# Routing weights by a one-hot product, and expert rows added into the stream by the fetches, in a two-layer kernel on one core

## The chip, the cores and the metric

The kernel runs on one core of one Trainium2 chip. The metric is the device time of one execution in microseconds. A core has TensorE (PE in the profile), VectorE (DVE), ScalarE (ACT), GpSimd (POOL) and SyncE (SP); SP, ACT and POOL issue DMAs, which all run on the core's 16 DMA engines.

## The reference, cut to what matters

Two different layers run one after the other over 1024 tokens of width 1024, in float32. The first ends in a mixture of experts with 16 experts in 4 groups; each token takes one group and two experts of it. The second begins with an RMS norm and the product with `w_in_2`.

```python
e_val = e_val / jnp.sum(e_val, -1, keepdims=True)
combine = one_hot(g_idx[:, 0], 4)[:, :, None] * g_val[:, :, None] * w_group[:, None, :]
hid = jax.nn.silu(gate) * up * combine[..., None]
moe = jnp.einsum('tef,efd->td', hid, w_down)
x = layer_norm(alpha * x + g_f * moe, ln2_g, ln2_b)       # end of the first layer
u = rmsnorm(x, norm_mix_2) @ w_in_2                       # start of the second
```

`g_f` is a row of 1024 gates that all tokens share; `alpha` is 2 to the power 1/4.

## The kernel before

The stream `x1` (tile arena_b) holds 8 tiles of 128 tokens by 1024. Each engine runs its own program, written out by hand in functions named after the engine, and the order on an engine is the order of the calls; between engines there are semaphores.

**The expert stage.** The router gives every token two places, one for each of its experts, in a list of 24 blocks ("slots") of 128 rows; a block belongs to one expert, or its two halves to two. `dve_router` works out the weights `w1` and `w2` (per token) and the places `posi`; `dve_inverse` and `pe_inverse` turn the places around by a product of two one-hot tables: `inv` names the token of each slot row. `pool_rows` fetches the rows of a block by an indirect DMA from a copy of the stream in DRAM, three blocks ahead (L1883). For each block TensorE turns the rows (L1954), multiplies by gate and up (L1966), turns the hidden tile (L1975) and multiplies by down (L1987). VectorE multiplies the result in PSUM by the gate row `rowg` (L2063), and ScalarE's queue stores it to `yslots` in DRAM (L2007). SP loads the experts' weights in three rotating buffers; the third gate and up buffer lies in arena_d, where the one-hot tables lie before, so SP waits for the tables' last use ahead of its third load (`if j == 2`).

**Adding the experts' rows.** When all blocks are stored, `pool_gather` fetches for each of the 8 token tiles the two rows of each token, 512 KB a fetch, into four buffers `g12` (L1896). ScalarE multiplies the second row by `w2` (L2104), VectorE adds the first times `w1` (L2159), then alpha times the stream (L2161). After that VectorE takes mean and variance (L1502 to L1505) and, one tile later, norms (L1510 to L1515), ScalarE sums squares (L2136), takes roots, and writes the normed tile `xr` (L2142), TensorE turns it (L1555), ScalarE copies it out (L2148). Meanwhile SP loads `w_in_2`, as soon as both rows of tile 1 are in (L2206), in two halves of 2 MB, and ScalarE multiplies each of their 16 pieces by `norm_mix_2` (L2117), two pieces a tile from the third turn of its loop on. In the second layer's first product (L2223) TensorE begins after the fifth turned tile and after the first eight pieces, one group of products a tile.

**GpSimd after that** builds tables for the second layer (`pool_tables`, L2604 to L2616), from the end of the last L2161 on.

## Time and profile before

| | us |
|---|---|
| median of 3 runs | 3191.38 (3189.43 to 3196.72) |
| the profiled execution, its own time | 3191.05 |
| its span in the profile | 3189.3 |
| PE busy | 2965.5 (93%) |
| DVE busy | 1505.0 (47%) |
| POOL busy | 1060.3 (33%) |
| ACT busy | 743.4 (23%) |
| mean granted TensorE clock | 0.961 |

The profile is of one execution. Its times count from the start of the span; 1.75 us of the execution lie outside it. Busy shares are means over stages with different limits: TensorE is full nearly everywhere, but two of its forty slices are low: the 21st (6 tenths), which holds the entry of the expert stage, and the 25th (2 tenths), which holds the addition of the experts' rows. A line such as "L2159 DVE" names the line of the kernel before. An indirect DMA of GpSimd shows as busy while its descriptors are written, not while data move.

### The profile page before, as it was taken

What the parts mean: (1) busy time and instruction counts of PE and PEld (TensorE: products, weight loads), DVE (VectorE), ACT (ScalarE), POOL (GpSimd) and SP (SyncE); (2) the same over time, 40 slices, a digit from 0 to 9 for tenths busy, and PEclk for the clock granted to TensorE, in tenths of its full rate; (3) what the DMA queues carried; (4) which work ended last, traced back from release to release, by engine and by line L of the source; (5) the groups of instructions that cost most, each with busy time, mean ns of one, the idle gap of its engine ahead of it and who ended that gap; (6) DMA issues with size and microseconds to landing.
All of it is one profiled execution on the core that took longest, in us unless ns stands there. A gap on an engine that the chain in (4) does not pass through costs nothing. (4 is left out here: it accounts for less than half of the span.)

```text
span 3189.3 us, 28756 instructions
## 1 busy us (share of the span) xinstructions
PE 2965.5 (93%) x10235; PEld 1480.4 (46%) x10235; DVE 1505.0 (47%) x2430; ACT 743.4 (23%) x1535; POOL 1060.3 (33%) x979
## 2 busy tenths in 40 slices
PE   7998999999899999999869992978999999999997
PEld 4554554444455555344534441565444444444443
DVE  2434882345666666322345327265132444444446
ACT  2213855411233333200111115222110000000002
POOL 0002870000376767500010003181022555555445
PEclk9998999999899999999979995998999999999998
DMA  7001322000100000111168964001020111211101
GB/s 268 20 0 52 88 79 96 27 27 19 34 1 1 1 1 1 54 33 37 49 252 339 391 269 165 4 14 53 0 79 27 40 40 40 73 46 40 40 14 60
DMA packets 128383, 229.14 MB, mean 72 GB/s; under 512 B 25288, under 2 KB 81264, under 8 KB 118384
## 3 DMA queue, kind: packets, MB, share of 16 engines
q1 hardware_dynamic: 117712, 197.72, 17.5%
q0 software_dynamic: 5760, 16.78, 1.4%
q10 hardware_dynamic: 4768, 12.79, 1.1%
q8 instruction: 82, 1.34, 0.2%
q14 instruction: 61, 0.50, 0.0%
HBM read 231.45 MB, written 22.03 MB: 79 GB/s over the span
## 5 line engine op out<-in xcount | busy, mean ns | idle before, releaser
L1366 DVE TENSOR_REDUCE arena_b<-ps 128x1 f32<-128x512 f32 (+1 forms) x384 | 217.6, 600 | 148.5 <-PE ps L1254 148.1
L3173 POOL TENSOR_TENSOR arena_b<-arena_b,arena_d 128x512 f32<-128x512 f32 x132 | 165.6, 1271 | 363.2 <-DVE arena_d L3353 362.2
L3325 DVE TENSOR_TENSOR arena_d<-arena_d,ps 128x512 f32<-128x512 f32 x154 | 101.8, 684 | 388.4 <-PE ps L3216 388.4
L1348 POOL TENSOR_TENSOR arena_b<-arena_b 128x512 f32<-128x512 f32 x182 | 224.5, 1268 | 96.6 <-ACT arena_b L1330 96.6
L1254 PE MATMUL ps<-arena_d,arena_a 64*128 64x512 f32 (+1 forms) x768 | 239.1, 548 | 3.7 <-DVE arena_b L1357 2.9
L1273 PE MATMUL ps<-arena_a,arena_d 64*128 64x512 f32 x640 | 220.0, 607 | 2.4 <-ACT arena_b L1330 1.8
L3350 DVE TENSOR_TENSOR arena_b<-arena_b,ps 128x512 f32<-128x512 f32 x264 | 174.3, 685 | 42.8 <-POOL arena_b L3173 27.4
L1077 PE MATMUL ps<-ring,arena_b 128*128 128x512 f32 x384 | 167.4, 592 | 0.0
L564 PE MATMUL ps<-arena_b,ring 128*128 128x512 f32 x384 | 167.1, 593 | 0.0
L1330 ACT ACTIVATE arena_b<-ps 128x512 f32<-128x512 f32 x214 | 116.2, 595 | 212.8 <-PE ps L1279 212.8
L3216 PE MATMUL ps<-arena_a,ring 128*128 128x512 f32 x352 | 155.1, 599 | 3.1 <-DMA ring<-in_w_up 3.1
L1254 PEld LDWEIGHTS ps<-arena_d,arena_a 64*128 64x128 f32 x768 | 115.2, 192 | 73.7 <-issue 42.5
L1966 PE MATMUL ps<-ring,arena_a 128*128 128x512 f32 (+1 forms) x352 | 144.2, 603 | 3.4 <-ACT arena_a L2014 3.4
L782 POOL TENSOR_TENSOR ring<-m_le,arena_t 128x512 f32<-128x512 f32 x32 | 40.7, 1271 | 285.8 <-ACT arena_d L654 282.1
L1348 POOL TENSOR_TENSOR arena_b<-arena_b,arena_t 128x512 f32<-128x512 f32 x96 | 118.8, 1269 | 46.1 <-ACT arena_t L1330 46.1
L1273 PEld LDWEIGHTS ps<-arena_a,arena_d 64*128 64x128 f32 x640 | 88.8, 185 | 79.4 <-issue 33.2
L3257 ACT ACTIVATE arena_d<-arena_d 128x512 f32<-128x512 f32 x44 | 27.8, 631 | 394.8 <-DVE arena_d L3325 394.8
L3237 PE MATMUL ps<-arena_c,arena_t 128*128 128x512 f32 x240 | 116.0, 592 | 0.0
L1484 PE MATMUL ps<-ring,arena_c 128*128 128x512 f32 x256 | 113.2, 595 | 0.0
L988 PE MATMUL ps<-ring,arena_b 128*128 128x512 f32 x256 | 112.3, 593 | 0.8 <-DVE arena_a L729 0.8
L564 PEld LDWEIGHTS ps<-arena_b,ring 128*128 128x128 f32 x384 | 72.0, 190 | 86.0 <-issue 86.0
L1077 PEld LDWEIGHTS ps<-ring,arena_b 128*128 128x128 f32 x384 | 71.7, 190 | 84.2 <-issue 84.2
(571 smaller groups left out, 5325.8 us busy)
## 6 DMA issues: line engine op xcount, KB each, us to landing
ring<-in_w_gate SPq DMA_DIRECT2D x33, 1024.0 KB
ring<-in_w_up SPq DMA_DIRECT2D x33, 1024.0 KB
ring<-in_w_down SPq DMA_DIRECT2D x33, 1024.0 KB
ring<-in_w_in SPq DMA_DIRECT2D x10, 2048.0 KB, 15.6
ring<-in_w_mod SPq DMA_DIRECT2D x32, 512.0 KB, 3.9
yslots<-arena_a ACTq DMA_DIRECT2D x24, 512.0 KB
arena_d<-in_w_gate SPq DMA_DIRECT2D x10, 1024.0 KB
arena_d<-in_w_up SPq DMA_DIRECT2D x10, 1024.0 KB
```

The costliest lines, as they stand in the source:

```text
L564: mm = eng.matmul(ps[:, b, 0:n], w[:, k, (m % 4) * P:(m % 4 + 1) * P], src[:, k, :], start=(k == 0), stop=(k == KT - 1))
L1077: mm = eng.matmul(ps[:, 2 * (j % 2) + n, :], h_tile(k, t), w[:, k, :], start=(k == 0), stop=(k == KT - 1))
L1254: eng.matmul(ps[:, shared("s", u), 0:k1 - k0], qT[rows, pr, q0:q0 + P], kT[rows, pr // 2, k0:k1], start=True, stop=True).then_inc(s_S, 1)
L1273: eng.matmul(ps[:, 3 + (n + e) % 3, :], kT[rows, pr // 2, kt * P:(kt + 1) * P], qT[rows, pr, qs], start=True, stop=False)
L1330: eng.activation(prT[n % NPR], ps[:, 3 + n % 3, :], ACT.Exp).then_inc(s_ex, 1)
L1348: eng.tensor_tensor(acc, first, prT[n % NPR], ALU.add).then_inc(s_pa, 1)
L1366: eng.tensor_reduce(mx3[j % 2][:, t, e, piece:piece + 1], ps[:, shared("s", u), 0:k1 - k0], AX.X, ALU.max).then_inc(s_mx, 1)
L1966: mm = eng.matmul(ps[c0:c1, s % 2, :], xsT[s % 2][:, k, c0:c1], sguw[j % 3][:, :, k, :], start=(k == 0), stop=(k == KT - 1))
L3173: eng.tensor_tensor(o, o, dsum[0 if a == "a12" else 1], ALU.add).then_inc(s_comb, 1)
L3216: mm = eng.matmul(bank_of("gu", b, w, p), lhs, rhs, start=(k == 0), stop=(k == HK - 1))
L3237: eng.matmul(bank_of("dn", b, i, p), lhs[p], rhs[p], start=True, stop=True).then_inc(dn_done, 1)
L3350: ins = eng.tensor_tensor(o, o, src, ALU.add)
```

## The change

The weights now enter at the experts' side. `dve_slot_weights` splits each token weight into three bfloat16 pieces and writes, for each piece, the one-hot table of blocks times the weight; `pe_slot_weights` multiplies by the one-hot table of rows (16 products that add up in one PSUM bank), and `dve_slot_weights_copy` adds the three pieces to `w_slot`, one weight for each slot row. The copy of a block's output (L2115 of after) multiplies by it and by the gate row in one instruction. SP's third load waits for the new product and not for `inv`.

The fetches write no buffers any more: each is an indirect DMA with an add, from `yslots` straight into the stream tile. GpSimd scales the eight stream tiles by alpha, one ahead of each of the row fetches 3 to 10. First rows of a tile are fetched three tiles ahead of second rows, since the two additions to one tile may not overlap. L2104, L2159 and L2161 are gone. SP's load of `w_in_2` still waits for both rows of tile 1, and GpSimd's tables now wait for the end of the expert products and the parameters alone.

```diff
+        def dve_slot_weights(eng):
+            place = Chain(eng, s_place, N_INV)
+            many = lambda v: v.rearrange("p j t n -> p (j t) n")
+            place(eng.tensor_copy(w_piece[0], w12))
+            place(eng.tensor_tensor(w_rest[0], w12, w_piece[0], ALU.subtract))
+            place(eng.tensor_copy(w_piece[1], w_rest[0]))
+            place(eng.tensor_tensor(w_rest[1], w_rest[0], w_piece[1], ALU.subtract))
+            place(eng.tensor_copy(w_piece[2], w_rest[1]))
+            for a in range(3):
+                place(eng.tensor_tensor(weight_of[:, :, a, :], many(slot_of), bc(w_piece[a], 2, NSLOT), ALU.mult))
+
+        def pe_slot_weights(eng):
+            eng.wait_ge(s_place, N_WT)
+            for j in range(2):
+                for t in range(LT):
+                    mm = eng.matmul(ps[:, 7, 0:3 * NSLOT], row_of[:, j, t, :],
+                                    weight_of[:, j * LT + t, :, :].rearrange("p a n -> p (a n)"),
+                                    start=(j + t == 0), stop=(j == 1 and t == LT - 1))
+            mm.then_inc(s_packT, 1)
+
+        def dve_slot_weights_copy(eng):
+            eng.wait_ge(s_packT, STRIP_SUM + NSTRIP + 4)
+            place(eng.tensor_copy(w_slot, ps[:, 7, 0:NSLOT]))
+            for a in (1, 2):
+                place(eng.tensor_tensor(w_slot, w_slot, ps[:, 7, a * NSLOT:(a + 1) * NSLOT], ALU.add))
...
         def pool_rows(eng):
+                if 3 <= n < 3 + LT:
+                    t = n - 3
+                    eng.tensor_scalar(x1[:, t, :], x1[:, t, :], ALPHA, None, ALU.mult).then_inc(s_gx, 1)
...
         def pool_gather(eng):
+            def rows_of(t, j):
+                return eng.indirect_dma_start(
+                    out=x1[:, t, :], out_offset=None, in_=yslots,
+                    in_offset=bass.IndirectOffsetOnAxis(ap=posi[:, j, t:t + 1], axis=0), compute_op=ALU.add)
+
+            eng.wait_ge(s_gx, LT)
             for i in range(2):
                 eng.wait_ge(ys_out[i], 16 * ((NSLOT + 1 - i) // 2))
-            for t in range(LT):
-                if t >= 4:
-                    eng.wait_ge(s_gx, t - 3)
-                for j in range(2):
-                    eng.indirect_dma_start(
-                        out=g12[t % 4][:, j, :], out_offset=None, in_=yslots,
-                        in_offset=bass.IndirectOffsetOnAxis(ap=posi[:, j, t:t + 1], axis=0)
-                    ).then_inc(g_in[t % 4], 16)
+            for u in range(LT + YLAG):
+                if u < LT:
+                    rows_of(u, 0).then_inc(g_in[u % 4], 16)
+                if u >= YLAG:
+                    t = u - YLAG
+                    eng.wait_ge(g_in[t % 4], 16 * (t // 4 + 1))
+                    if t >= 3:
+                        eng.wait_ge(*second_rows(t - 3))
+                    rows_of(t, 1).then_inc(y_in[t % 3], 16)
...
                 if j == 2:
-                    eng.wait_ge(s_place, N_INV)
+                    eng.wait_ge(s_packT, STRIP_SUM + NSTRIP + 4)
...
-                eng.tensor_tensor(ysl[s % 2], ps[:, 5:7, :].rearrange("p a n -> p (a n)"), rowg, ALU.mult
-                                  ).then_inc(s_ye, 1)
+                eng.scalar_tensor_tensor(out=ysl[s % 2], in0=ps[:, 5:7, :].rearrange("p a n -> p (a n)"),
+                                         scalar=w_slot[:, ORDER[s]:ORDER[s] + 1], in1=rowg, op0=ALU.mult,
+                                         op1=ALU.mult).then_inc(s_ye, 1)
...
-        def act_second_row(eng, t):
-            eng.wait_ge(g_in[t % 4], 32 * (t // 4 + 1))
-            eng.activation(g12[t % 4][:, 1, :], g12[t % 4][:, 1, :], ACT.Identity, scale=w2[:, t:t + 1]
-                           ).then_inc(s_re, 1)
...
         def dve_x2(eng):
-                    g = g12[t % 4]
-                    eng.wait_ge(s_re, row_scaled(t))
-                    ch = Chain(eng, s_place, N_INV + t)
-                    ch(eng.scalar_tensor_tensor(out=g[:, 0, :], in0=g[:, 0, :], scalar=w1[:, t:t + 1], in1=g[:, 1, :],
-                                                op0=ALU.mult, op1=ALU.add))
-                    step(eng, eng.scalar_tensor_tensor(out=x1[:, t, :], in0=x1[:, t, :], scalar=ALPHA, in1=g[:, 0, :],
-                                                       op0=ALU.mult, op1=ALU.add), s_gx, t + 1)
+                    eng.wait_ge(*second_rows(t))
...
         def sp_second(eng):
-            eng.wait_ge(g_in[1], 32)
+            eng.wait_ge(*second_rows(1))
...
         def pool_tables(eng):
-            eng.wait_ge(s_gx, LT)
+            after(eng, "moe")
```

GpSimd's program where the experts' rows are fetched, before. "slot_rows_stored" is the landing of the blocks in DRAM, "experts_added" the end of an L2161.

```order
L1896 DMA arena_d<-yslots,arena_t 128x1024 [waits slot_rows_stored1,slot_rows_stored0]
L1896 DMA arena_d<-yslots,arena_t 128x1024 x3
L1896 DMA ring<-yslots,arena_t 128x1024 x4
L1896 DMA arena_d<-yslots,arena_t 128x1024 [waits experts_added]
L1896 DMA arena_d<-yslots,arena_t 128x1024
L1896 DMA arena_d<-yslots,arena_t 128x1024 [waits experts_added]
```

And in the changed kernel. "first_rows_added" is the landing of a first row, "slot_and_second_rows_loaded" that of a second.

```order
L1936 DMA arena_b<-yslots,arena_t 128x1024 [waits slot_rows_stored1,slot_rows_stored0,stream_tiles_scaled]
L1936 DMA arena_b<-yslots,arena_t 128x1024 x3
L1936 DMA arena_b<-yslots,arena_t 128x1024 [waits first_rows_added0]
L1936 DMA arena_b<-yslots,arena_t 128x1024
L1936 DMA arena_b<-yslots,arena_t 128x1024 [waits first_rows_added1]
L1936 DMA arena_b<-yslots,arena_t 128x1024
L1936 DMA arena_b<-yslots,arena_t 128x1024 [waits first_rows_added2]
```

The first four fetches are first rows of tiles 0 to 3; the second row of tile 1 was the fourth fetch and is the seventh, and fetches wait for fetches, not for VectorE.

VectorE's program in the same stage, tiles 1 and 2 (with the norm of tile 0), before:

```order
L2159 SCALAR_TENSOR_TENSOR arena_d<-arena_d,arena_t 128x1024 [waits router_act_steps,norm_steps]
L2161 SCALAR_TENSOR_TENSOR arena_b<-arena_b,arena_d 128x1024 [waits place_steps]
L1502 BN_STATS arena_d<-arena_b 128x6 [waits experts_added]
L1502 BN_STATS arena_d<-arena_b 128x6
L1504 BN_AGGR arena_d<-arena_d 128x2 [waits norm_steps]
L1505 TENSOR_SCALAR arena_d<-arena_d 128x1 [waits norm_steps]
L1510 RECIPROCAL arena_d<-arena_d 128x1 [waits conditions_and_roots,norm_steps]
L1513 SCALAR_TENSOR_TENSOR arena_b<-arena_b,arena_d 128x1024 [waits norm_rows_loaded,normed]
L1515 SCALAR_TENSOR_TENSOR arena_b<-arena_b,arena_d 128x1024 [waits normed]
L2159 SCALAR_TENSOR_TENSOR ring<-ring,arena_t 128x1024 [waits router_act_steps,normed]
```

And in the changed kernel:

```order
L1502 BN_STATS arena_d<-arena_b 128x6 [waits slot_and_second_rows_loaded1,norm_steps]
L1502 BN_STATS arena_d<-arena_b 128x6
L1504 BN_AGGR arena_d<-arena_d 128x2 [waits norm_steps]
L1505 TENSOR_SCALAR arena_d<-arena_d 128x1 [waits norm_steps]
L1510 RECIPROCAL arena_d<-arena_d 128x1 [waits conditions_and_roots,norm_steps]
L1513 SCALAR_TENSOR_TENSOR arena_b<-arena_b,arena_d 128x1024 [waits norm_rows_loaded,normed]
L1515 SCALAR_TENSOR_TENSOR arena_b<-arena_b,arena_d 128x1024 [waits normed]
L1502 BN_STATS arena_d<-arena_b 128x6 [waits slot_and_second_rows_loaded2,normed]
```

Two of the big instructions of a tile are gone, and the statistics wait for the DMA itself.

VectorE's program between its parameter steps and the first expert block, before:

```order
L2445 TENSOR_SCALAR arena_c<-arena_c 128x32 [waits s5_param_steps]
L2043 TENSOR_SCALAR arena_a<-ps,csil 128x128 [waits slot_rows_turned,rope_loaded,s5_param_steps]
L2043 TENSOR_SCALAR arena_a<-ps,csil 128x128 x3
L2051 TENSOR_TENSOR arena_a<-arena_a,ps 128x256 [waits silu_ready]
```

And in the changed kernel:

```order
L1728 CAST arena_d<-arena_t 128x16 [waits s5_param_steps]
L1729 TENSOR_TENSOR arena_d<-arena_t,arena_d 128x16 [waits place_steps]
L1730 CAST arena_d<-arena_d 128x16 [waits place_steps]
L1731 TENSOR_TENSOR arena_d<-arena_d 128x16 [waits place_steps]
L1732 CAST arena_d<-arena_d 128x16 [waits place_steps]
L1734 TENSOR_TENSOR arena_d<-arena_d 128x16x24 [waits place_steps] x3
L2095 TENSOR_SCALAR arena_a<-ps,csil 128x128 [waits slot_rows_turned,rope_loaded,place_steps]
L2095 TENSOR_SCALAR arena_a<-ps,csil 128x128 x3
L1749 COPY arena_t<-ps 128x24 [waits small_products]
L1751 TENSOR_TENSOR arena_t<-arena_t,ps 128x24 [waits place_steps] x2
L2103 TENSOR_TENSOR arena_a<-arena_a,ps 128x256 [waits silu_ready,place_steps]
```

Eight steps stand ahead of the first block's modulation and three behind it.

## Rows read from the trace of the kernel before

**Rows 1.** Stretches: start:end, length, busy (x) of PE, PEld, DVE, ACT, POOL; PEclk, DMA share, GB/s.
```profile
1915.00:1947.50 32.50, 0.00 (x0) 0.00 (x0) 20.54 (x29) 9.66 (x14) 13.15 (x14) 0.54 0.86 324
1947.50:1980.00 32.50, 9.84 (x40) 7.84 (x40) 31.02 (x48) 23.75 (x39) 2.95 (x8) 0.50 0.21 80
1980.00:2012.00 32.00, 31.67 (x88) 15.05 (x88) 6.74 (x14) 15.41 (x25) 21.94 (x38) 0.96 0.04 9
2012.00:2107.00 95.00, 94.32 (x248) 59.63 (x248) 25.94 (x28) 17.90 (x30) 30.07 (x68) 1.00 0.00 1
```

**Rows 2.** Waits of PE from 1622 to 2107: us in total, times, longest us.
```profile
PE ps L1555 <- ACT arena_t L2142: 55.8, 5, 33.5
```

**Rows 3.** Timeline of DVE, one tile: start us, us, line, operation [idle before].
```profile
1960.77 1.28 DVE L2159 SCALAR_TENSOR_TENSOR arena_d<-arena_d,arena_t 128x1024 f32<-128x1024 f32 x1
1962.08 1.23 DVE L2161 SCALAR_TENSOR_TENSOR arena_b<-arena_b,arena_d 128x1024 f32<-128x1024 f32 x1
1963.34 1.28 DVE L1502 BATCH_NORM_STATS2 arena_d<-arena_b 128x6 f32<-128x512 f32 x2
...
1968.32 1.28 DVE L2159 SCALAR_TENSOR_TENSOR ring<-ring,arena_t 128x1024 f32<-128x1024 f32 x1
```

**Rows 4.** Timeline of ACT and PE up to the second layer's first product.
```profile
1947.54 1.32 ACT L2117 ACTIVATE ring<-ring,cols 128x512 f32<-128x512 f32 x2
...
1964.78 1.15 ACT L2104 ACTIVATE ring<-ring,arena_t 128x1024 f32<-128x1024 f32 x1
...
1968.12 1.06 ACT L2136 ACTIVATE arena_t<-arena_b 128x1024 f32<-128x1024 f32 x1 [2.01 <-DVE arena_b L1515]
...
1980.04 8.44 PE L2223 MATMUL ps<-arena_a,ring 128*128 128x512 f32 x16 [0.15 <-ACT arena_a L2148]
```

**Rows 5.** Timeline of POOL and SP at the fetches, and landing of L1896.
```profile
1918.86 0.95 POOL L1896 DMA_INDIRECT arena_d<-yslots,arena_t  x1 [58.13 <-DMA yslots<-arena_a]
1920.12 0.95 POOL L1896 DMA_INDIRECT arena_d<-yslots,arena_t  x1 [0.30 <-issue]
...
1928.87 1.07 SPq L2208 DMA_DIRECT2D ring<-in_w_in  x2
...
DMA to landing us min/median/max: 4.2/6.3/8.3
```

**Rows 6.** DMA from 1930 to 1933, then 1933 to 1942; queues: packets, MB, share.
```profile
DMA packets 348, 1.20 MB, mean 399 GB/s; under 512 B 36, under 2 KB 36, under 8 KB 348
q1 hardware_dynamic: 39, 0.08, 6.8%
...
DMA packets 1317, 3.65 MB, mean 405 GB/s; under 512 B 64, under 2 KB 64, under 8 KB 1316
q0 software_dynamic: 588, 2.15, 60.1%
q1 hardware_dynamic: 728, 1.49, 43.2%
```

**Rows 7.** Timeline at the entry of the expert stage: DVE, PE and SP.
```profile
1607.19 1.15 DVE L1706 TENSOR_TENSOR arena_d<-arena_d 128x384 bf16<-128x384 f32 x2
1610.92 0.50 PE L1722 MATMUL ps<-arena_d 128*128 128x48 bf16 x8 [0.76 <-DVE arena_d L1708]
1613.08 0.34 SPq L1925 DMA_DIRECT2D arena_d<-in_w_gate  x1
1617.17 0.18 DVE L2445 TENSOR_SCALAR arena_c<-arena_c 128x32 f32<-128x32 f32 x1
1622.17 1.95 PE L1954 MATMUL ps<-ident,arena_a 128*128 128x128 f32 x8 [8.63 <-DMA arena_a<-x_dram,arena_t]
1638.17 0.62 PE L1966 MATMUL ps<-ring,arena_a 128*64 128x512 f32 x1 [1.69 <-ACT arena_a L2014]
```

**Rows 8.** Timeline of DVE beside POOL, and POOL's waits from 1625 to 1915.
```profile
1984.89 1.36 DVE L1513 SCALAR_TENSOR_TENSOR arena_b<-arena_b,arena_d 128x1024 f32<-128x1024 f32 x1
1997.75 1.04 POOL L2611 TENSOR_TENSOR ring<-ring,arena_c 128x512 f32<-128x512 f32 x1
...
POOL arena_a L1883 <- PE ps L1954: 223.3, 21, 13.2
```

More of the change, by code:

```diff
@@ L1667, in build @@
         inv = view(arena_t, 3440, NSLOT).bitcast(U32)
+        w12 = view(arena_t, 3864, 2 * LT)
+        w_piece = [view(arena_d, 3600 + 8 * i, 8).bitcast(BF16) for i in range(3)]
+        w_rest = [view(arena_d, 3632 + 16 * i, 2 * LT) for i in range(2)]
+        weight_of = view(arena_d, LT * P, 3 * LT * NSLOT).bitcast(BF16).rearrange("p (m a n) -> p m a n", a=3, n=NSLOT)
+        w_slot = view(arena_t, 3520, NSLOT)
+        N_WT = N_INV + 8
+        N_WS = N_WT + 3
         def pool_places(eng):
@@ L1716, in dve_inverse_copy @@
             place(eng.tensor_copy(posi, posf))
+        def dve_slot_weights(eng):
[8 more added lines that the diff above has]
+                place(eng.tensor_tensor(weight_of[:, :, a, :], many(slot_of), bc(w_piece[a], 2, NSLOT), ALU.mult))
+            assert place.n == N_WT
+        def pe_slot_weights(eng):
[7 more added lines that the diff above has]
+        def dve_slot_weights_copy(eng):
+            place = Chain(eng, s_place, N_WT)
+            eng.wait_ge(s_packT, STRIP_SUM + NSTRIP + 4)
+            place(eng.tensor_copy(w_slot, ps[:, 7, 0:NSLOT]))
+            for a in (1, 2):
+                place(eng.tensor_tensor(w_slot, w_slot, ps[:, 7, a * NSLOT:(a + 1) * NSLOT], ALU.add))
+            assert place.n == N_WS
         def pe_inverse(eng):
@@ L1863, in parts @@
                 [(LOADS.index((n, 0)), 0, P)]
-        g12 = [view(a, at, 2, D) for a, at in ((arena_d, 0), (arena_d, 2 * D), (ring, 2 * PAN), (ring, 2 * PAN + 2 * D))]
-        xs_in = [sem(f"slot_rows_loaded{i}") for i in range(3)]
+        xs_in = [sem(f"slot_and_second_rows_loaded{i}") for i in range(3)]
+        y_in = xs_in
         ys_out = [sem(f"slot_rows_stored{i}") for i in range(2)]
-        g_in = [sem(f"token_rows_gathered{i}") for i in range(4)]
+        g_in = [sem(f"first_rows_added{i}") for i in range(4)]
         s_xT, s_xe = sem("slot_rows_turned"), sem("slot_rows_modulated")
         s_hT, s_hTc = sem("slot_hidden_turned"), sem("slot_hidden_copied")
-        s_ye, s_gx = sem("slot_output_copied"), sem("experts_added")
+        s_ye, s_gx = sem("slot_output_copied"), sem("stream_tiles_scaled")
         ends["moe"] = [(dn_done, NSLOT)]
@@ L1887, in pool_rows, with second_rows @@
                 ).then_inc(xs_in[n % 3], 16)
+        YLAG = 3
+        def second_rows(t):
+            return y_in[t % 3], 16 * (NSLOT // 3) + 16 * (t // 3 + 1)
         def pool_gather(eng):
+            def rows_of(t, j):
[3 more added lines that the diff above has]
+            eng.wait_ge(s_gx, LT)
             for i in range(2):
                 eng.wait_ge(ys_out[i], 16 * ((NSLOT + 1 - i) // 2))
-            for t in range(LT):
-                if t >= 4:
-                    eng.wait_ge(s_gx, t - 3)
-                for j in range(2):
-                    eng.indirect_dma_start(
-                        out=g12[t % 4][:, j, :], out_offset=None, in_=yslots,
-                        in_offset=bass.IndirectOffsetOnAxis(ap=posi[:, j, t:t + 1], axis=0)
-                    ).then_inc(g_in[t % 4], 16)
+            for u in range(LT + YLAG):
[7 more added lines that the diff above has]
+                    rows_of(t, 1).then_inc(y_in[t % 3], 16)
         def sp_ln2(eng):
@@ L2062, in store @@
                     eng.wait_ge(ys_out[s % 2], 16 * (s // 2))
-                eng.tensor_tensor(ysl[s % 2], ps[:, 5:7, :].rearrange("p a n -> p (a n)"), rowg, ALU.mult
-                                  ).then_inc(s_ye, 1)
+                eng.scalar_tensor_tensor(out=ysl[s % 2], in0=ps[:, 5:7, :].rearrange("p a n -> p (a n)"),
+                                         scalar=w_slot[:, ORDER[s]:ORDER[s] + 1], in1=rowg, op0=ALU.mult,
+                                         op1=ALU.mult).then_inc(s_ye, 1)
+            dve_slot_weights(eng)
             eng.wait_ge(s_rope, 32 + 32)
             modulate(0)
+            dve_slot_weights_copy(eng)
             hidden(0)
@@ L2100, in build @@
         s_xr = sem("stream_normed")
-        def act_second_row(eng, t):
-            eng.wait_ge(g_in[t % 4], 32 * (t // 4 + 1))
-            eng.activation(g12[t % 4][:, 1, :], g12[t % 4][:, 1, :], ACT.Identity, scale=w2[:, t:t + 1]
-                           ).then_inc(s_re, 1)
-        def row_scaled(t):
-            return 2 + t + 1 + 2 * max(0, t - 3)
-        IN2_GAINED = (2 + LT - 1 + KT, 2 + LT + 2 * KT)
+        IN2_GAINED = (2 + KT, 2 + 2 * KT)
         def act_gains(eng, n, k):
@@ L2119, in act_x2 @@
         def act_x2(eng):
-            eng.wait_ge(s_place, N_PLACE)
-            act_second_row(eng, 0)
             for t in range(LT + 3):
-                if t + 1 < LT:
-                    act_second_row(eng, t + 1)
                 if t < LT:
@@ L3509, in _ @@
             pe_s5_params(eng)
+            pe_slot_weights(eng)
             pe_slots(eng)
```

## The prediction

> **What bounds the kernel now.** I read the stage table first, then the waits of TensorE, then the timeline of the one stretch that they point to. In the stage table [rows 1] TensorE does nothing from 1915.0 to 1947.5, works 9.84 of the next 32.5 us, and from 1980.0 on is full again (31.67 of 32.0, then 94.32 of 95.0). The waits say the same: 55.8 us in five pieces, 33.5 us the longest, all for ScalarE's L2142, which writes the normed stream [rows 2]. So between the last expert block and the first product of the second layer (L2223, 1980.04) time is set by something else, and whatever moves that product moves everything behind it, since TensorE hardly waits for 127 us after.
>
> Inside the gap two things matter. VectorE turns one tile every 7.55 us (L2159 at 1960.77 and again at 1968.32 [rows 3]), with no idle time between. And the DMA engines are full: at 405 GB/s from 1933 to 1942 [rows 6]. They carry 16 fetches of 512 KB (8.39 MB) and then w_in_2, twice 2.10 MB, which ScalarE must multiply by the norm gains (L2117) before TensorE may use it. L2117 first runs at 1947.54, without idle time ahead of it [rows 4]: before, those weights are in time.
>
> **What the change takes away.** On VectorE L2159 and L2161 go: start to start 1.31 and 1.26 us [rows 3], so a tile takes 7.55 - 2.57 = 4.98 us. On ScalarE L2104 (1.15 us a tile [rows 4]) goes. ScalarE's tile was its 7.55 less 2.0 of idle [rows 4], and is now some 4.5 us, still under VectorE. Were nothing else to change, four tile turns lie between the first gain and the first product (32.5 us = 4 x 7.55 + 2.3), so 10 us would go there, and some more ahead of it.
>
> **What the fetches now cost.** The two rows of a token are no longer copied into a buffer but added into the stream by the DMA. The trace has no adding DMA; its price is bounded by the plain fetch. 0.524 MB at the 399 GB/s of 1930 to 1933 [rows 6] is 1.31 us of all DMA engines. A plain fetch reads a row and writes a row. An added one reads two rows (the expert's and the stream's own) and writes one. If the second read is free it stays 1.31 us; if reading is the full side, it is 2.62; if the three passes follow each other, 3.93. I take 2.62: the plain fetch already keeps the engines full with one read, so the second needs the same time again. Both ends stay in the range. It can't be under 1.31, as no byte is saved.
>
> The Trainium skill bears on this (Collectives: The Full Stack, "The bandwidth ceiling: the fold count and why AG ≠ RS ≠ AR"): an add in the DMA reads two sources through the same read ring, and the measured collective with adds ran at about half the rate of the copying one. No row of this trace shows it. By that rule a fetch is 2.62 us and the time 3197, by the plain row 1.31 us and 3180 (both worked out below).
>
> **When w_in_2 arrives.** It is issued when both rows of tile 1 are in. Before, that was 1928.87, and its first bytes moved about 3.6 us later (39 packets by 1933 [rows 6]). Now tile 1's second row is the seventh fetch in GpSimd's new order (four first rows, then second and first rows in turn). The first fetch is issued at 1918.86 and a plain one lands after 4.2 at best [rows 5]; with 1.31 more it lands at 1924.4. Six more at 2.62 give 1940.1. First bytes: 1943.7. GpSimd's own issuing is no limit: 1.25 us a fetch [rows 5].
>
> Then w_in_2 shares the engines with the fetches that are left. In 1933 to 1942 it had 43.2% and the fetches 60.1% [rows 6], normed 42 to 58, with 728 packets of 2 KB against 588, most of 4 KB. So engines take packets from both queues nearly in turn, and a packet that costs double takes double: 42 to 116, or 27% for the weights. The Trainium skill (DMA: Bandwidth & Descriptors, "Queues, rings and completion order") says the same, that an engine goes round the queues packet by packet; the packet counts agree. The first half of w_in_2 needs 2.10 MB at 405 GB/s, 5.2 us, alone, so 19.3 us, and about 1 to land: **1964.0**. By then five more fetches have passed, tile 4's second row among them; the last row lands near 1972, and VectorE and ScalarE need it later than that.
>
> **From there to the product.** ScalarE is in order, so it stands at L2117 until 1964.0, and VectorE with it, one tile on, at the root that ScalarE would take next. From the first gain to the product: 4 x 4.98 + 2.3 = 22.2, less 1.2 since VectorE stands ahead: 21.0. First product: 1985.0, against 1980.04. **+5.0 us.**
>
> **Smaller terms.** GpSimd's tables (from L2604) waited for the last L2161 and now start once the last fetch is issued, beside VectorE's norms. Where they meet, L1513 takes 1.36 us and not 1.28, and large table steps take 1.04 [rows 8]. Eight to ten such meetings: +0.8. The store of an expert block takes a scalar more; only the last is on the path, +0.05. GpSimd scales eight stream tiles between row fetches, 1 to 2.5 us each by its 1.04 for half a tile [rows 8]. It waited 223.3 us in 21 pieces there [rows 8], 10.6 each, and rows are fetched three blocks ahead: nothing.
>
> At the entry VectorE has five small steps (0.2 each) and three products of 384 elements (0.57, as L1706) after its last parameter step at 1617.35: done at 1620.1. Then 16 small products on TensorE, 0.50 for eight narrower ones [rows 7], so 1.3: 1621.5. The first turn waits for its rows until 1622.17 [rows 7]. The row fetch covers it with 0.7 us to spare; with no cover at all it would cost the whole 4.2. SP is moved more: the third weight buffer, and down weights queued behind it, wait for those products, 1621.6 and not 1613.08. Its 2.10 MB at three quarters of the engines are in at 1631; TensorE takes them at 1638.17 [rows 7]. Nothing, with 7 us to spare.
>
> **Sum.** 3191.05 (the profiled execution, 0.33 under the median of the runs) + 5.0 + 0.8 + 0.1 = **3197**.
>
> **Rivals.**
> *An added fetch costs what a plain one does.* The first lands at 1923.1, the seventh at 1931, first bytes of w_in_2 at 1934.5, 5.2 / 0.42 = 12.4 and 1 more: 1947.9, product at 1968.9: 11 us less, **3180**. For it: writes are not more than before, and the full engines may be full on the writing side. Against it: two reads.
> *In between*, two reads partly beside each other, 1.97 a fetch: first in at 1923.7, seventh 1935.5, bytes 1939.1, share 42 to 87 or 33%, weights at 1955.9, product at 1977: **3189**, and 3183 to 3194 on either side.
> *Half rate, but the queues share time, not packets:* weights at 1957; now the rows are late, 4.5 us a fetch, tile 6 complete near 1974, product near 1983: **3194**. Against it the packet counts.
> *Slower for certain: an added fetch costs more than two reads.* At 3.93: first in at 1925.7, seventh 1949.3, bytes 1952.9, share 42 to 174 or 19%, weights in 27 + 1 us later at 1980.7, product 2001.7: **3213**. From about 2.7 us a fetch on, the loss passes 0.2%. A variant is that the issue itself grows past 2.6 us on GpSimd.
> *The change doesn't do what it says:* the weighting isn't hidden at the entry, TensorE's small products or the third weights come late and hold the first two blocks. That adds 1 to 7 to the sum: 3198 to 3204.
>
> **How the numbers follow.** Half rate in either sharing 0.42 (3194 to 3200, 3197 likeliest), copy rate 0.24 (3180), between 0.14, above half 0.16 (3201 to 3225), the entry 0.04. A measurement of this kernel can tell about 0.2%, 6.4 us. Faster than that: the copy rate and half of the between, 0.31. Slower: all above half, 0.35 of the half-rate case and the entry, 0.34. Within: 0.35. The range reaches from the copy rate, 3179, to three passes, 3213.
>
> **What the profile after would show.** VectorE's tile turns at 4.98 us once nothing waits. The queue of GpSimd: about 200 GB/s alone, 400 if the first rival holds. The landing of an added fetch: 5.5 us for the first. w_in_2 issued near 1940. ScalarE idle ahead of its first gain, ended by a DMA, until about 1964. First product of the second layer at 1985, and the stretch behind it as long as before. If ScalarE isn't idle ahead of the gain, the DMA term is wrong and the time is near 3180; if VectorE waits for rows on every tile, it is above 3200.

## The result and the profile after

| | before | after |
|---|---|---|
| median of 5 runs, us | 3194.38 (3189.43 to 3197.63) | 3207.61 (3205.43 to 3210.08) |
| the profiled execution, us | 3191.05 | 3205.43 |
| mean granted TensorE clock | 0.961 | 0.959 |

The changed kernel takes 1.0044 times as long (95% interval 1.0032 to 1.0055): slower by some 13 to 14 us, where the prediction had 6 (3197 against 3191.05).

The waits of TensorE from 1700 to 2000 (us in total, times, longest) and the stretches of the core, with the columns of [rows 1]:

```profile
PE ps L1555 <- ACT arena_t L2184: 69.3, 5, 39.8
```

```profile
1915.00:1970.40 55.40, 1.97 (x8) 1.57 (x8) 16.19 (x29) 5.44 (x11) 30.58 (x41) 0.53 0.95 212
1970.40:1993.90 23.50, 7.92 (x33) 6.32 (x33) 20.83 (x36) 19.31 (x36) 18.70 (x20) 0.50 0.16 60
...
2026.60:2121.60 95.00, 94.32 (x248) 59.61 (x248) 25.95 (x28) 17.94 (x29) 30.48 (x69) 1.00 0.00 1
```

The first line answers to [rows 2]: the same wait, 69.3 us and not 55.8. The last answers to the last of [rows 1]: behind the gap nothing has changed, 94.32 of 95 us. In the first 55 us after the last block the DMA engines are full (0.95) and move only 212 GB/s, where before it was 324 at 0.86.

The chain through the gap, on POOL, SP, ACT, DVE and PE (timelines; L2163 is the gain, L2259 the first product of the second layer):

```profile
1919.34 1.59 POOL L1936 DMA_INDIRECT arena_b<-yslots,arena_t  x1 [58.27 <-DMA yslots<-arena_a]
```

```profile
1942.24 2.23 SPq L2244 DMA_DIRECT2D ring<-in_w_in  x2
```

```profile
1970.37 1.33 ACT L2163 ACTIVATE ring<-ring,cols 128x512 f32<-128x512 f32 x2 [16.00 <-DMA ring<-in_w_in]
```

```profile
1937.22 1.29 DVE L1502 BATCH_NORM_STATS2 arena_d<-arena_b 128x6 f32<-128x512 f32 x2 [21.29 <-DMA arena_b<-yslots,arena_t]
1942.27 1.29 DVE L1502 BATCH_NORM_STATS2 arena_d<-arena_b 128x6 f32<-128x512 f32 x2 [3.33 <-DMA arena_b<-yslots,arena_t]
...
1971.99 0.16 DVE L2210 RECIPROCAL qss<-qss 128x1 f32<-128x1 f32 x1 [13.24 <-ACT qss L2172]
```

```profile
1993.86 5.33 PE L2259 MATMUL ps<-arena_a,ring 128*128 128x512 f32 x8 [0.15 <-ACT arena_a L2190]
```

ScalarE, which had no idle time ahead of its first gain [rows 4], now stands 16.00 us for `w_in_2`, and VectorE 13.24 us behind it. Before that, VectorE waits 21.29 us for the first tile's rows.

The stretch ahead of the expert stage varies by some us from execution to execution (the stage's first product lies between 1603.6 and 1611.8 in the kernels below), in code that none of them changes. So I cut the profiles at events: the stage's first product (L1722 before, L1758 after), the start of the last copy of a block (L2063, L2115), VectorE's L1502 on the first and on the eighth tile, and the first product of the second layer. All lengths are in us; the ratio is that of the times to those of the kernel before, run beside it.

| kernel | first product to last copy | to the first L1502 | to the eighth | to the product | last copy to product | ratio (95% interval) |
|---|---|---|---|---|---|---|
| before | 304.58 | 14.77 | 49.44 | 1.59 | 65.80 | 1 |
| after | 307.14 | 22.57 | 52.47 | 4.17 | 79.21 | 1.0044 (1.0032 to 1.0055) |
| e1_plain | 306.95 | 16.42 | 36.18 | 4.16 | 56.76 | 0.9971 (0.9959 to 0.9982) |
| e2_early | 306.97 | 27.74 | 34.94 | 4.16 | 66.84 | 0.9993 (0.9984 to 1.0003) |
| e3_tables | 307.00 | 21.82 | 49.87 | 4.17 | 75.86 | 1.0031 (1.0015 to 1.0046) |
| e4_noscale | 306.19 | 23.01 | 52.59 | 4.16 | 79.76 | 1.0028 (1.0015 to 1.0041) |
| e9_parta | 306.22 | 13.64 | 48.85 | 1.65 | 64.14 | 0.9988 (0.9978 to 0.9997) |
| e6b_alladd | 304.79 | 22.85 | 38.30 | 4.16 | 65.31 | 0.9995 (0.9986 to 1.0004) |
| e8b_hybrid | 304.74 | 13.75 | 41.68 | 2.90 | 58.33 | 0.9972 (0.9961 to 0.9982) |
| e10_before_early | 305.99 | 15.30 | 49.43 | 1.58 | 66.31 | 1.0000 (0.9991 to 1.0009) |
| e11_mix | 304.73 | 13.91 | 38.63 | 4.17 | 56.71 | 0.9969 (0.9957 to 0.9981) |
| e12_hold | 307.08 | 22.50 | 52.50 | 4.17 | 79.17 | 1.0043 (1.0028 to 1.0059) |
| e13_again (before once more) | 306.12 | 15.03 | 49.44 | 1.59 | 66.06 | one run |

For after: +2.56 in the first column and +13.41 from the last copy to the product, 15.97 in all. The stage began 2.15 us earlier than before and the part behind the product is 0.58 longer, which gives the 14.4 us between the two profiled executions.

### The profile page after: what moved, and what is told of

Read it like the earlier page. It is cut to its first block and busy times, and to the rows that moved or that the text cites. A ratio compares the mean times of both kernels' runs of the same rounds, so it can differ in the third digit from the quotient of the medians.

```text
span 3203.7 us, 28788 instructions
## 1 busy us (share of the span) xinstructions
PE 2970.0 (93%) x10251; PEld 1483.0 (46%) x10251; DVE 1492.8 (47%) x2425; ACT 734.2 (23%) x1527; POOL 1093.2 (34%) x987
```

## The experiments

The kernels are variants of the changed kernel where nothing else is said.

### What an adding fetch costs: e1_plain

```diff
-                    in_offset=bass.IndirectOffsetOnAxis(ap=posi[:, j, t:t + 1], axis=0), compute_op=ALU.add)
+                    in_offset=bass.IndirectOffsetOnAxis(ap=posi[:, j, t:t + 1], axis=0))
```

> The changed kernel with the add taken out of its 16 fetches (they overwrite the stream tile, so the sum over experts is left out); order, waits and everything else stay. Theory A, the second read of an adding fetch is what costs: the queue of GpSimd goes back from 210 to about 400 GB/s, w_in_2 is issued near 1931 and its first gain runs near 1948, the second layer's first product comes 21 to 24 us earlier than in the changed kernel (1993.9), and the ratio to the kernel before is 0.997 to 0.998. Rival B, the new order (first rows three tiles ahead, tile 1's second row seventh) is what costs: the first gain stays past 1962 and the ratio above 1.002.

Measured: 3181.9 us, product 56.8 us behind the last copy. The adding fetches of after against the plain ones here, in the same order: landing in us of the 16 (minimum, median, maximum), and three microseconds in which the fetches have the DMA engines to themselves (queue: packets, MB, share of the engines' time; a share at or a little over 100% is read as full).

After, 1936 to 1939:

```profile
DMA to landing us min/median/max: 6.3/12.0/17.6
...
DMA packets 170, 0.63 MB, mean 209 GB/s; under 512 B 17, under 2 KB 17, under 8 KB 170
...
q0 software_dynamic: 170, 0.63, 105.7%
```

e1_plain, 1927 to 1930:

```profile
DMA to landing us min/median/max: 4.2/6.7/8.1
...
DMA packets 334, 1.21 MB, mean 403 GB/s; under 512 B 39, under 2 KB 39, under 8 KB 334
...
q0 software_dynamic: 334, 1.21, 100.2%
```

With the engines full in both, an adding fetch of 0.524 MB at 209 GB/s is 2.5 us of all engines, a plain one at 403 GB/s 1.3. So the add doubles a fetch, and that one argument is worth 22.4 us from the last copy to the product (79.21 less 56.76): the whole loss of the change and all that it could have gained. The rule of the Trainium skill that the prediction set beside its sum (Collectives: The Full Stack, two source reads through one ring and so half the rate) fits: 209 against 403 is half the rate. That it is the second read which takes the time is not shown; the run shows the price of the add as a whole.

### When w_in_2 is loaded: e2_early, e10_before_early

e2_early issues `w_in_2` as soon as the last expert product is done:

```diff
-            eng.wait_ge(*second_rows(1))
```

> The changed kernel with w_in_2 issued as soon as the last expert product is done, and not behind both rows of tile 1. Theory A, ScalarE and VectorE stand because w_in_2 shares the DMA engines with adding fetches and gets a quarter of them: no idle time ahead of the first gain, the expert rows come up to 10 us later, first product at 1977 to 1982 instead of 1993.9, ratio to before 0.999 to 1.002. Rival C, the rows themselves are what is late: the product moves by less than 4 us and the ratio stays at 1.004.

Measured: 3188.91 us, 66.84 us from copy to product, 12.4 less than after. ScalarE no longer idles ahead of the gain, and VectorE runs at 4.98 us a tile from the third tile on, as the prediction worked out for tiles that wait for nothing:

```profile
1939.94 1.29 DVE L1502 BATCH_NORM_STATS2 arena_d<-arena_b 128x6 f32<-128x512 f32 x2 [26.45 <-DMA arena_b<-yslots,arena_t]
1945.01 1.29 DVE L1502 BATCH_NORM_STATS2 arena_d<-arena_b 128x6 f32<-128x512 f32 x2 [3.36 <-DMA arena_b<-yslots,arena_t]
1949.96 1.29 DVE L1502 BATCH_NORM_STATS2 arena_d<-arena_b 128x6 f32<-128x512 f32 x2 [0.39 <-DMA arena_b<-yslots,arena_t]
1954.96 1.29 DVE L1502 BATCH_NORM_STATS2 arena_d<-arena_b 128x6 f32<-128x512 f32 x2
1959.93 1.29 DVE L1502 BATCH_NORM_STATS2 arena_d<-arena_b 128x6 f32<-128x512 f32 x2
```

But the first tile comes 5.2 us later than in after (27.74 against 22.57). The 4 MB run beside the store of the last block, and the first fetch is issued 10.45 us behind the last copy and not 4.7. The cost of the load has not gone; it has moved to that store, for which the fetches wait.

e10_before_early shows that the load alone was worth nothing before. It is the kernel before with the first half of `w_in_2` issued at the last use of its place in the ring, some 30 us earlier:

```diff
+            eng.wait_ge(gu_done, max(LOADS[j][0] for j in range(len(LOADS)) if j % 3 == 0) + 1)
+            eng.dma_start(slot(0), panel_of(w_in2, 0, 0)).then_inc(s_w2[0], 16)
             after(eng, "moe")
             eng.wait_ge(g_in[1], 32)
-            for n in range(2):
-                eng.dma_start(slot(n), panel_of(w_in2, 0, HALF * n)).then_inc(s_w2[n], 16)
+            eng.dma_start(slot(1), panel_of(w_in2, 0, HALF)).then_inc(s_w2[1], 16)
```

> The kernel before with the first half of w_in_2 issued as in the two previous ones. Theory A: there VectorE sets the pace and the weights were in time (landed 16.3 us behind their issue, 2.3 us ahead of the first gain), so nothing changes but a microsecond or two from fetches with less company: ratio 0.999 to 1.001. Rival G, the early load is itself the gain of the other two: ratio under 0.998.

Measured: 3191.26 us beside 3190.28. The gap is 66.31 us against 65.80 and 66.06, with VectorE at 7.55 us a tile. Before, VectorE's own work bounds the gap; only the change makes it depend on the load.

### Why the first half of w_in_2 lands so late: e12_hold

In after it lands 28.1 us behind its issue, where the prediction had 23.9.

```diff
             for n in range(2):
+                if n:
+                    eng.wait_ge(s_w2[0], 16)
                 eng.dma_start(slot(n), panel_of(w_in2, 0, HALF * n)).then_inc(s_w2[n], 16)
```

> The changed kernel, with the second half of w_in_2 issued only when the first has landed. It tells why the first half landed 28.1 us behind its issue and not about 20 to 24. Theory: each DMA engine works through its own list, and some engines lag with the adding fetches; the second half's packets ran on engines that had finished the first half and cost the lagging ones nothing. Then the first half still lands 26 to 28.5 us behind its issue, the product stays within 2 us of 79.2 behind the last block's copy, and the time is 0 to 4 us from that of the changed kernel, later if anything, since the second half is late. Rival: the second half's bytes took the first's turns. Then it lands in 20 to 24 us and the product comes 4 to 7 us earlier.

Measured: 3204.91 us. The first half alone lands after 27.8 us (it is the maximum of the two landings), so the second half took nothing from it. Queues of this kernel from 1958 to 1962, 1962 to 1966 and 1966 to 1970:

```profile
q0 software_dynamic: 176, 0.64, 80.0%
q1 hardware_dynamic: 172, 0.35, 25.9%
```

```profile
q1 hardware_dynamic: 326, 0.65, 44.1%
```

```profile
q0 software_dynamic: 125, 0.44, 55.9%
q1 hardware_dynamic: 36, 0.06, 4.8%
```

The packets go one to one (176 and 172), and the weights get 26% of the engines' time, as the prediction had it (27%). But they move less in that time than it reckoned. After itself, from 1950 to 1962, with both queues busy throughout:

```profile
q0 software_dynamic: 526, 1.90, 79.5%
q1 hardware_dynamic: 527, 1.08, 26.5%
```

1.08 MB in 12 us is 90 GB/s, and 2.10 MB at that rate take 23.3 us; the prediction's 19.3 us are 109 GB/s, that is 27% of the full rate of 405. In the 26.5% of the time that they have, the weights move at 340 GB/s: a packet holds an engine for 97 ns (26.5% of 16 x 12 us, over 527), and before it was 85 (43.2% of 16 x 9 us, over 728, [rows 6]). With 4.2 us from the issue to the first bytes (25 packets by 1947) that makes 27.5, and it lands after 28.1. By 1964.0, when the forecast had all of it in, 1.56 MB are through.

The end is less even. In e12_hold the weights run at 0.24 MB a microsecond from 1964 to 1966, when the fetches run low, and 2.04 of the 2.10 MB are through by 1966, 24.0 us behind the issue; the last 36 packets take until 1969.8, while fetches still move. So some engines end early and some late, and the transfer is done when its slowest engine is. That the late ones are engines which never ran out of adding packets is argued from the numbers, not seen, since the records do not give me the engine of each packet. The Trainium skill (DMA: Bandwidth & Descriptors, "Why a DMA increments its semaphore by 16 and not by 1") has each engine report its own part, and all data landed only with the last; a late tail of 36 packets fits that.

### GpSimd's tables beside the norms: e3_tables

```diff
-            after(eng, "moe")
+            eng.wait_ge(s_l1, 2 * LT * N_L1)
```

> The changed kernel with GpSimd's tables put behind the last norm of the expert stage, so that they meet none of VectorE's norms. Theory A: L1513 and L1515 go back to 1.28 us each, the time from the first gain to the first product falls from 23.5 to about 21.0 us, ratio to before 1.0036 to 1.0038. Rival D, nothing is gained because ScalarE is the one that sets the pace there: 23 us and more, or the tables are missed later and the stretch behind the product grows.

Measured: 3199.75 us. The stretch from gain to product is 20.93 us and not 23.49. The norm steps of VectorE in the same place, first after (beside the tables), then e3_tables:

```profile
1981.07 1.95 DVE L1515 SCALAR_TENSOR_TENSOR arena_b<-arena_b,arena_d 128x1024 f32<-128x1024 f32 x1
...
1985.39 2.08 DVE L1513 SCALAR_TENSOR_TENSOR arena_b<-arena_b,arena_d 128x1024 f32<-128x1024 f32 x1
```

```profile
1979.43 1.29 DVE L1513 SCALAR_TENSOR_TENSOR arena_b<-arena_b,arena_d 128x1024 f32<-128x1024 f32 x1
1980.76 1.28 DVE L1515 SCALAR_TENSOR_TENSOR arena_b<-arena_b,arena_d 128x1024 f32<-128x1024 f32 x1
```

So the tables cost 2.6 us where they were booked at 0.8. The six norm steps between the gain and the product of after take 10.28 us together, and at 1.28 each they would take 7.68: that is the 2.6. The Trainium skill (SBUF — State Buffer, "SBUF: two separate sides") says that a VectorE operation with two SBUF inputs and a GpSimd operation that reads SBUF exclude each other on a port pair for a whole instruction. The trace agrees in kind: L1513 and L1515 have two, the table steps read SBUF, and the norm steps take up to 0.8 us more.

### GpSimd's scaling in the block loop: e4_noscale, e13_again

e4_noscale scales 8 of the 1024 columns of each stream tile, so 1016 columns of the stream enter the sum unscaled.

```diff
-                    eng.tensor_scalar(x1[:, t, :], x1[:, t, :], ALPHA, None, ALU.mult).then_inc(s_gx, 1)
+                    eng.tensor_scalar(x1[:, t, 0:8], x1[:, t, 0:8], ALPHA, None, ALU.mult).then_inc(s_gx, 1)
```

> The changed kernel with GpSimd's scaling by alpha cut to 8 of 1024 columns of each stream tile (the rest of the stream is left unscaled). Theory A, the scaling meets VectorE's small parameter steps behind the first expert block, TensorE then waits 3.3 us and not 2.4 and its granted clock falls for some 5 us: the block loop from the first turned tile to the last store takes 292 us as before and not 294.4, ratio to before 1.0036 to 1.0038. Rival E, the 2.3 us in the loop are a matter of the single execution or of the block output's copy: the loop stays at 294 us.

Measured: 3201.35 us, loop 306.19 us against 307.14 of after and 304.58 of before. The scaling costs 0.9 us, through one wait of TensorE for VectorE's hidden tile (after, then e4_noscale: total, times, longest):

```profile
PE ps L2039 <- DVE arena_c L2109: 5.3, 3, 3.3
```

```profile
PE ps L2039 <- DVE arena_c L2109: 4.5, 3, 2.4
```

VectorE's small parameter steps run beside the scaling at 1655: eight take 2.65 us and not 1.83, and the scaling of a tile takes GpSimd 2.77.

That leaves 1.6 us in the loop. e13_again runs the kernel before once more:

> The kernel before, unchanged, once more. If the lower granted clock near 1660 us is a matter of the single execution and not of the change, this profile may or may not show it, and the stretch from the first product of the expert stage to the last block's copy is then either 304.6 (no dip) or 306.0 us (dip), and nothing else; the first product itself may lie 2 to 6 us off 1609.66, since that varied over the kernels in code that none of them changes.

Its loop is 306.12 us. The stretches at this place, e13_again and then after (the granted clock is the third number from the end):

```profile
1655.00:1660.00 5.00, 5.00 (x16) 1.60 (x14) 1.21 (x4) 0.00 (x0) 0.00 (x0) 0.66 0.22 73
```

```profile
1655.00:1660.00 5.00, 1.74 (x11) 1.06 (x11) 4.64 (x16) 1.54 (x5) 3.85 (x2) 0.92 0.26 105
1660.00:1665.00 5.00, 5.00 (x16) 1.73 (x13) 0.96 (x3) 0.00 (x0) 0.00 (x0) 0.73 0.24 75
```

And the kernel before at that place, in its first execution:

```profile
1655.00:1660.00 5.00, 3.02 (x15) 1.86 (x13) 4.32 (x21) 1.89 (x5) 0.99 (x1) 1.00 0.57 238
```

Behind the longest of those waits the granted clock falls from its upper level (2.4 GHz) towards the lower for a few microseconds, in this execution of the unchanged kernel and not in the first one (1.00 throughout). The lengths fall into three groups: 304.6 to 304.8 (before, e6b_alladd, e8b_hybrid, e11_mix), 306.0 to 306.2 with the dip (e13_again, e10_before_early, e9_parta, e4_noscale), and 307.0 to 307.1 with the dip and the scaling (after, e1_plain, e2_early, e3_tables, e12_hold). So the dip costs 1.4 us and comes in one execution and not in another. All five profiles with the scaling have it, and four of the eight without.

That does not yet make the scaling its cause. The two kinds of execution differ already at the stage's first product, some 15 us ahead of GpSimd's first scaling (1622.30 in after). Before, then e13_again:

```profile
1609.66 0.50 PE L1722 MATMUL ps<-arena_d 128*128 128x48 bf16 x8 [9.06 <-DVE arena_d L1708]
```

```profile
1604.26 0.50 PE L1722 MATMUL ps<-arena_d 128*128 128x48 bf16 x8 [9.27 <-DVE arena_d L1708]
```

TensorE idles 9.03 to 9.06 us there in the four profiles without the dip, and 9.27 to 9.37 in the nine with it. So the dip goes with something that stands before any of the changed code has run. Thirteen profiles do not prove that it decides alone, and what it is stays open.

### Each half of the change alone, and better versions: e9_parta, e6b_alladd, e8b_hybrid, e11_mix

e9_parta keeps the weighting by the one-hot product and fetches plainly into four buffers, with two additions on VectorE and no scaling on GpSimd:

```diff
+                    ch(eng.tensor_tensor(g[:, 0, :], g[:, 0, :], g[:, 1, :], ALU.add))
+                    step(eng, eng.scalar_tensor_tensor(out=x1[:, t, :], in0=x1[:, t, :], scalar=ALPHA, in1=g[:, 0, :],
+                                                       op0=ALU.mult, op1=ALU.add), s_gx, t + 1)
```

> One part of the change alone: the weights enter in the copy of a block's output, but the fetches are plain ones into four buffers as in the kernel before; VectorE adds the two rows and then alpha times the stream (two instructions, as before), ScalarE has no row to scale, GpSimd scales nothing. Theory A, this part is hidden and the adding fetch is all of the loss: from the place products to the second layer's first product 368 to 371 us (370.4 before, 386.4 changed), ratio 0.998 to 1.001. Rival F, the entry or the block copy costs by itself: 372 us and more.

Measured: 3185.9 us, ratio 0.9988. From copy to product it is 64.14 us, 1.7 to 1.9 less than before: the first L1502 comes 1.1 to 1.4 earlier, with ScalarE's L2104 gone ahead of it, and VectorE's tile takes 7.49 us and not 7.55. Its loop has the dip and nothing else. The weighting is free, and the loss of the change lies in the fetches with the add and what comes with them.

e6b_alladd keeps all adding fetches and mends what surrounds them: the first half of `w_in_2` early as in e10_before_early, tables late as in e3_tables, scaling on ScalarE in the block loop:

```diff
+                if 1 <= s < 1 + LT:
+                    eng.activation(x1[:, s - 1, :], x1[:, s - 1, :], ACT.Identity, scale=ALPHA).then_inc(s_gx, 1)
```

> The changed kernel with three moves: the first half of w_in_2 is issued as soon as its place in the ring was last read (in the last blocks, where the DMA engines are nearly idle), GpSimd's tables wait for the last norm, and the scaling by alpha goes to ScalarE. Theory A: no idle time of ScalarE ahead of its first gain, the pace is that of the second rows (5.0 us a tile), first product 58 to 61 us behind the last store's start (65.8 before, 79.2 changed), ratio to before 0.997 to 0.999. Rival C, the rows are late anyway: 64 us and more, ratio 1.000 or above.

Measured: 3190.18 us, no difference from before, 65.31 us from copy to product. ScalarE now finds its weights in (gain at 1955.25 without idle time), and yet:

```profile
1938.20 1.28 DVE L1502 BATCH_NORM_STATS2 arena_d<-arena_b 128x6 f32<-128x512 f32 x2 [21.57 <-DMA arena_b<-yslots,arena_t]
1943.23 1.28 DVE L1502 BATCH_NORM_STATS2 arena_d<-arena_b 128x6 f32<-128x512 f32 x2 [3.32 <-DMA arena_b<-yslots,arena_t]
...
1954.97 1.29 DVE L1502 BATCH_NORM_STATS2 arena_d<-arena_b 128x6 f32<-128x512 f32 x2 [1.65 <-DMA arena_b<-yslots,arena_t]
1961.56 1.29 DVE L1502 BATCH_NORM_STATS2 arena_d<-arena_b 128x6 f32<-128x512 f32 x2 [1.64 <-DMA arena_b<-yslots,arena_t]
```

My forecast of 58 to 61 us missed the start. The first tile's second row is the fifth fetch, at 2.5 us each, so the first L1502 comes 22.85 us behind the last copy, 8 later than before. The pace gives 11.1 back (38.30 against 49.44), 2.6 more go since the product then follows the eighth tile by 4.16 and not 1.59. Even without any wait for `w_in_2`, and with the tables and the scaling out of the way, the adding fetches only break even.

So e8b_hybrid, otherwise as e6b_alladd, takes one of a tile's two rows plainly, into eight buffers that VectorE adds, and the other with the add. Two rows of a tile then no longer exclude each other, and go out one behind the other:

```diff
+            for t in range(LT):
...
+                eng.indirect_dma_start(
+                    out=g8[t], out_offset=None, in_=yslots,
+                    in_offset=bass.IndirectOffsetOnAxis(ap=posi[:, 0, t:t + 1], axis=0)).then_inc(g_in[t % 4], 16)
...
+                rows_of(t, 1).then_inc(y_in[t % 3], 16)
...
+                    step(eng, eng.tensor_tensor(x1[:, t, :], x1[:, t, :], g8[t], ALU.add), s_gx, LT + t + 1)
```

> As the previous one, but of a tile's two rows only one is added by its fetch; the other is fetched plainly into one of eight buffers and added by VectorE (one product-free add, 1.25 us a tile). 16 fetches then take 8 x 1.31 + 8 x 2.5 = 30.5 us of the DMA engines and not 40, and no fetch waits for the one before it. Theory A: VectorE's tile 6.2 us, first rows in 12 us behind the first issue, first product 56 to 58 us behind the last store's start, ratio 0.9965 to 0.9985. Rival C: mixing both kinds keeps the queue at the slow rate, 61 us and more.

Measured: 3182.86 us beside 3190.28, ratio 0.9972. The first L1502 comes 13.75 us behind the last copy (e6b_alladd: 22.85), and from the third tile on each follows the last by 6.23 us, which is 4.98 and one addition of 1.26, with no idle time. This beats both kernels.

e11_mix does the same for tiles 0 to 3 alone; tiles 4 to 7 get both rows by adding fetches.

```diff
+                    if t < 4:
+                        eng.wait_ge(g_in[t], 16)
+                        step(eng, eng.tensor_tensor(x1[:, t, :], x1[:, t, :], g8[t], ALU.add), s_gx, LT + t + 1)
```

> The hybrid again, but with plain first rows (into buffers, added by VectorE) for tiles 0 to 3 alone; tiles 4 to 7 get both rows by adding fetches. Theory: with tile 0 early, VectorE's own pace sets the product: tiles 0 to 3 at 6.23 us, the rest at 4.98, so four additions of 1.26 fewer ahead of the product, 58.3 behind the last block's copy becomes 53 to 54, ratio to before 0.9945 to 0.9965. Rival: the DMA engines set it. 4 plain fetches of 1.31 and 12 adding ones of 2.5 with half of w_in_2 (5.2) are 40.5 us from the first issue; the last tiles then have VectorE waiting by 1 to 4 us each on tiles 4 to 7, and the product is 56 to 60 behind the copy, ratio 0.9965 to 0.998.

Measured: 3180.37 us beside 3190.27, ratio 0.9969; from e8b_hybrid it can't be told apart. The gap is 56.71 us: 1.6 less, not 5, and within the rival's 56 to 60. Of the 5.0 us of additions saved, 2.0 go to one wait for tile 4's rows and 1.3 to the longer way from the eighth L1502 to the product (4.17 against 2.90):

```profile
1951.81 1.29 DVE L1502 BATCH_NORM_STATS2 arena_d<-arena_b 128x6 f32<-128x512 f32 x2 [2.00 <-DMA arena_b<-yslots,arena_t]
```

## Why the prediction was right in kind and short in size

The mechanism held step by step: a fetch with an add takes twice a plain one's share of the DMA engines, `w_in_2` is issued later for it, gets 27% of the engines beside it, and ScalarE and VectorE stand until it lands. The time, 3207.6, lies within 3179 to 3213, but 10.6 us over the point. 3.0 of that are the runs of the kernel before, 3194.4 beside it and 3191.4 in the forecast; in the ratio it is 1.0044 against 1.0019.

That the range holds the result is in part luck. The prediction gave half rate 3194 to 3200, and times from 3201 on to a fetch dearer than two reads, with a chance of 0.16; the fetch cost 2.5 us, less than two reads, and the time still came out at 3207.6, from terms that the forecast had at less or at nothing. It tied a loss of over 0.2% to a fetch of over 2.7 us, and to the change as a whole it gave a chance of 0.34 of being slower by that much, no more than to faster (0.31) or neither (0.35). Two rivals' sums are rounded down (3180.8 and 3213.6 by their own terms, for 3180 and 3213), which changes nothing.

- **The price of a fetch.** Forecast 2.62 us, measured 2.5 (209 GB/s). The rival of the copy rate, 3180 us, falls; e1_plain, which has that rate, takes 3181.9.
- **The issue of w_in_2.** Forecast 21.2 us behind the first fetch, measured 22.9: the first lands after 6.3 and not 5.5, six more take 16.6 and not 15.7.
- **Its arrival.** Forecast 1964.0, measured 1970.4. The later start and issue account for 2.1 of that, the rest is the landing, 28.1 for 23.9. The share of the engines' time was right. The step that failed is the time made of it, "5.2 us, alone, so 19.3 us": 27% of 405 GB/s is 109, and beside the adding packets the weights moved at 90, which makes 23.3 us. The first bytes took 4.2 us and not 3.6. For "about 1 to land" 0.6 is left by this count; e12_hold shows that it is a tail of late packets and no fixed term.
- **From the gain to the product.** Forecast 21.0 and 0.8 for the tables; measured 23.5. Without the meetings it is 20.93 (e3_tables), so the 21.0 was right and the tables were mis-sized: 2.6. The row behind the 0.8 [rows 8] showed one meeting of 1.36 us with small tables; the larger ones, which take GpSimd 1.04 us and more, now fall on the norms.
- **The block loop.** Booked at nothing, measured +2.3. Of it 0.9 is GpSimd's scaling: the prediction asked whether GpSimd has time for it, which it has, and not what VectorE does beside it. The other 1.4 is the dip of the clock, which the unchanged kernel has too in e13_again and not in its first execution; it is not shown to be the change's.
- **The entry.** Forecast hidden, and it was: the 16 products take 1.14 us and the first turn still waits 1.27 us for its rows; it costs 0.2. The third weights are issued at 1619.9, 6.9 us later by the profile and 9.0 later counted from the stage's first product, and nothing waits for them. The copy of a block takes 1.28 and not 1.23, as booked. Behind the product nothing moved, as forecast.

In sum: +5.9 forecast between the stage's first product and the second layer's, +16.0 measured. The 10 us between them are 5.9 for the arrival counted from the first fetch, 1.7 for the tables beyond the 0.8, 2.3 for the loop (1.4 of it the dip) and 0.2 for the entry.

What the prediction did not see at all, because the wait for `w_in_2` lay over it: with the adding fetches the first tile is ready 8 us later. e6b_alladd, where that wait is gone, shows it. So loading in another order takes the loss away and leaves no gain: of the 11.1 us that VectorE's shorter tile gives there, 8.1 go to the later first tile and 2.6 to the longer way behind the eighth.

## What to carry to other kernels

A DMA that adds into SBUF is not an addition for free: here it cost 1.2 us of all DMA engines for each 0.5 MB more than a plain one, about what VectorE takes for the same addition (1.26 us), so it pays only where the DMA engines have that time. Price it by the first tile as well as by the pace: what must be fetched twice into the same place, one behind the other, delays the first tile by every fetch ahead of it, and one plain and one adding fetch a tile was the better split. Take a load beside slow packets at the rate that it has there, and not as its share of the full one: here it had 26% of the engines' time, and 90 GB/s of 405. And look what an engine that is moved beside VectorE does to VectorE's steps, not only whether it has the time.

## What the runs showed of the hardware that I had not expected

- GpSimd's own issue of an adding fetch takes 1.55 us against 0.94 for a plain one (the 16 of L1936 in after and in e1_plain), so 1.85 from one to the next and not 1.25. It is hidden here behind 2.5 us of transfer.
- A load beside adding fetches, packet for packet, moved at 90 GB/s with 26.5% of the engines' time, and each of its packets held an engine for 97 ns where it was 85 beside plain ones.
- The last 36 packets, 3% of a load, came up to 3.8 us behind the rest of it (e12_hold).
- The same program had the dip of the clock near 1656 us in one execution and none in another, at a cost of about 1.5 us (e13_again, 306.12 against 304.58).
- VectorE's operations on two SBUF tensors took up to 2.08 us and not 1.28 beside GpSimd's tables, well over the 1.36 of [rows 8].
